# One new order of finer stages in the attention phase of a hybrid encoder block

## What is computed

```
h = rms_norm(x); q, k, v, p = h @ W_in              # 512, 128, 128, 512 columns
q, k = rms_norm(q), rms_norm(k)                     # per head of 64
a = attention(q, k, v, sinks)                       # window of 128, chunks of 64, a sink per head
m = (trailing means of p over 2, 4, 8, 16, minus p) @ pool_w, scaled
x = x + concat([a, m]) @ W_out
u = causal_conv3(rms_norm(x) @ W_up)                # 2 x 2816 columns
x = x + (silu(u_gate) * u_value) @ W_down
```

## Time and profile before

| | us |
|---|---|
| median of 3 executions | 1937.17 (1935.85 to 1940.52) |
| profiled execution | 1936.87 |
| its span, first to last instruction | 1935.0 |
| TensorE busy | 1788.9, 92% of the span |
| VectorE busy | 1350.6, 70% |
| ScalarE busy | 872.2, 45% |
| GpSimd busy | 244.5, 13% |
| mean granted TensorE clock | 0.966 |

### The profile page before, as it was taken

How to read it: one execution, slowest core, us unless ns; L and a number is a source line. 1 busy time by engine, 2 the same in 40 slices (tenths; PEclk the granted TensorE clock), 3 DMA queues, 4 the chain that set the end, 5 groups by cost and what they waited for, 6 DMA issues and landing times.

```text
span 1935.0 us, 23457 instructions
## 1 busy us (share of the span) xinstructions
PE 1788.9 (92%) x8490; PEld 1488.2 (77%) x8490; DVE 1350.6 (70%) x1786; ACT 872.2 (45%) x1499; POOL 244.5 (13%) x278
## 2 busy tenths in 40 slices
PE   5779979979976599999999999999999899999999
PEld 5668867768865488888888788888887688888887
DVE  4464454454532698989998889888897777775784
ACT  5454563663553444444445444444443433333331
POOL 1211211211111300000000000000001212220110
PEclk9989989989988699999999999999999899999999
DMA  5232244234443434243235622222223799885884
GB/s 182 66 124 72 66 163 142 66 121 141 142 154 139 151 132 142 68 140 120 88 122 192 227 91 77 88 77 87 85 79 112 261 377 318 288 296 174 295 298 148
DMA packets 218563, 295.51 MB, mean 153 GB/s; under 512 B 12937, under 2 KB 120145, under 8 KB 218449
## 3 DMA queue, kind: packets, MB, share of 16 engines
q1 hardware_dynamic: 199009, 239.49, 38.4%
q10 hardware_dynamic: 19440, 54.53, 7.2%
HBM read 234.20 MB, written 59.77 MB: 152 GB/s over the span
## 4 chain that ended last, share of the span: by engine, by line
PE 71%; DMA 9%; DVE 8%; ACT 7%; issue 3%; POOL 1%; SPq 1%; ACTq 0%; DVEq 0%; POOLq 0%
PE ps L625 23%; PE ps L627 23%; PE ps L626 23%; DMA dg<-gT_d 4%; ACT xs L972 2%; DMA h2T_d<-hs 1%; DMA dw<-in_w_down_dram 1%; ACT junk L884 1%; PE ps L663 1%; ACT n L896 1%; DVE ds_lo L1554 1%; DVE cb L1439 1%; DMA x_d<-r 1%; ACT r L1004 1%; ACT w_hi L866 1%
## 5 line engine op out<-in xcount | busy, mean ns | idle before, releaser
L625 PE MATMUL ps<-va_hi,wv 128*128 128x512 f32 x1232 | 483.5, 392 | 46.3 <-DVE va_lo L1387 30.8
L627 PE MATMUL ps<-va_hi,wv 128*128 128x512 f32 x1232 | 482.4, 392 | 0.0
L626 PE MATMUL ps<-va_lo,wv 128*128 128x512 f32 x1232 | 482.3, 391 | 0.0
L625 PEld LDWEIGHTS ps<-va_hi,wv 128*128 128x128 f32 x1232 | 233.4, 189 | 96.5 <-DVE va_lo L1387 31.7
L627 PEld LDWEIGHTS ps<-va_hi,wv 128*128 128x128 f32 x1232 | 233.1, 189 | 49.0
L626 PEld LDWEIGHTS ps<-va_lo,wv 128*128 128x128 f32 x1232 | 233.5, 190 | 48.4
L625 PE MATMUL ps<-dt_hi,ds_hi 128*128 128x512 f32 x616 | 239.7, 389 | 0.1
L627 PE MATMUL ps<-dt_hi,ds_lo 128*128 128x512 f32 x616 | 239.6, 389 | 0.0
L626 PE MATMUL ps<-dt_lo,ds_hi 128*128 128x512 f32 x616 | 239.6, 389 | 0.0
L1439 DVE SCALAR_TENSOR_TENSOR cb<-ub,cst,cb 128x1024 f32<-128x1024 f32 x176 | 218.8, 1286 | 7.5 <-ACT cb L1069 7.5
L1202 DVE TENSOR_TENSOR w_lo<-raw,w_hi 128x1024 fp32r<-128x1024 f32 x72 | 96.4, 1348 | 136.4 <-ACT w_hi L866 135.9
(11 more groups left out here) (158 smaller groups left out, 2923.1 us busy)
## 6 DMA issues: line engine op xcount, KB each, us to landing
dg<-gT_d SPq DMA_DIRECT2D x264, 256.0 KB, 5.0
rw<-in_w_up_dram SPq DMA_DIRECT2D x84, 512.0 KB, 5.1
dw<-in_w_down_dram SPq DMA_DIRECT2D x132, 256.0 KB, 5.4
gT_d<-cb ACTq DMA_DIRECT2D x44, 512.0 KB, 2.6
raw<-in_w_in_dram SPq DMA_DIRECT2D x40, 512.0 KB, 3.8
raw<-in_w_out_dram SPq DMA_DIRECT2D x32, 512.0 KB, 3.9
n<-in_x_dram SPq DMA_DIRECT2D x16, 512.0 KB, 5.8
x_d<-r ACTq DMA_DIRECT2D x16, 512.0 KB, 3.2
```

What stands on the lines that cost most here:

```text
L625: pe.matmul(out_ap, l_hi, r_hi, start=first, stop=False, skip_group_check=True)
L626: pe.matmul(out_ap, l_hi, r_lo, start=False, stop=False, skip_group_check=True)
L627: return pe.matmul(out_ap, l_lo, r_hi, start=False, stop=last, skip_group_check=True)
```

## The change

`ORDER` is written anew. n1 and n2 become two stages each: n1sq, n2sq (squares, stores, inverse roots) and n1sc, n2sc (the scaling, now `tensor_scalar` on VectorE). t1 is taken in halves and t2 in quarters j of two feature tiles. The inverse sums leave s for a stage inv; ScalarE's copy of sp is a stage pt; the key and value work of kv is a stage kve. join waits for o(1, 1) instead of o(1, 3). The first block is turned tile by tile into all eight banks as each tile is scaled, and its products start after one feature tile instead of five. o waits for the attention half only at k = 2. VectorE adds before it splits. The seven small vectors are loaded from ScalarE's queue instead of SP's.

```diff
     units("n1", 0, ())
-    units("t1", 0, ())
+    units("t1", 0, (0,))
     for g in range(4):
...
             units("win", 0, (g,))
+    units("kv", 0, (0,), (1,))
+    units("kve", 0, ())
     for a in range(NB):
         more, back = a + 1 < NB, a > 0
-        units("kv", a, (0,), (1,))
+        if a > 1:
+            units("kv", a, (0,))
+            units("t2", a - 2, (2,))
+            units("kv", a, (1,))
+            units("kve", a, ())
+            units("t2", a - 2, (3,))
+        units("q", a, (0,))
         units("pm", a, (0,), (1,))
         units("win", a, (2,))
-        units("q", a, (0,))
+        if more:
+            units("n1sq", a + 1, ())
+        units("q", a, (1,))
         units("pm", a, (2,))
         units("win", a, (3,))
-        units("q", a, (1,), (2,))
+        if more:
+            units("n1sc", a + 1, ())
+        units("q", a, (2,))
         units("pm", a, (3,))
...
             units("kt", a, ())
-            units("n1", a + 1, ())
-            units("t1", a + 1, ())
+            units("t1", a + 1, (0,), (1,))
             units("qt", a, ())
...
             units("win", a + 1, (0,))
+            units("inv", a, (0,))
             units("pin", a + 1, (1,))
+            units("s", a, (2,), (3,))
             units("win", a + 1, (1,))
-            units("s", a, (2,), (3,))
             units("pin", a + 1, (2,))
+            units("inv", a, (1,))
+            units("pin", a + 1, (3,))
             units("sp", a, (0,), (1,))
-            units("pin", a + 1, (3,))
+            units("pt", a, (0,), (1,))
+            units("kv", a + 1, (0,))
             units("av", a, (0,), (1,))
             units("sp", a, (2,), (3,))
+            units("pt", a, (2,), (3,))
+            units("kv", a + 1, (1,))
             units("av", a, (2,), (3,))
+            units("kve", a + 1, ())
             continue
...
         units("o", a - 1, (1, 0))
-        if more:
-            units("n1", a + 1, ())
+        units("inv", a, (0,))
         units("o", a - 1, (1, 1))
         units("s", a, (2,), (3,))
+        units("join", a, ())
         units("o", a - 1, (1, 2), (1, 3))
-        units("join", a, ())
+        units("inv", a, (1,))
         if more:
-            units("t1", a + 1, ())
-            units("n2", a - 1, ())
+            units("t1", a + 1, (0,))
+            units("sp", a, (0,))
+            units("t1", a + 1, (1,))
+            units("sp", a, (1,))
+            units("pt", a, (0,), (1,))
             units("pin", a + 1, (0,))
-            units("sp", a, (0,), (1,))
+            units("n2sq", a - 1, ())
             units("win", a + 1, (0,))
+            units("av", a, (0,), (1,))
             units("pin", a + 1, (1,))
-            units("av", a, (0,), (1,))
+            units("n2sc", a - 1, ())
             units("win", a + 1, (1,))
+            units("sp", a, (2,), (3,))
+            units("pt", a, (2,), (3,))
             units("pin", a + 1, (2,))
-            units("sp", a, (2,), (3,))
+            units("av", a, (2,), (3,))
+            units("t2", a - 1, (0,))
             units("pin", a + 1, (3,))
-            units("t2", a - 1, ())
-            units("av", a, (2,), (3,))
-        else:
-            units("sp", a, (0,), (1,))
-            units("av", a, (0,), (1,))
-            units("sp", a, (2,), (3,))
-            units("n2", a - 1, ())
-            units("av", a, (2,), (3,))
+            units("t2", a - 1, (1,))
     last = NB - 1
-    units("o", last, (0, 0), (0, 1))
-    units("t2", last - 1, ())
+    units("sp", last, (0,), (1,))
+    units("pt", last, (0,), (1,))
+    units("n2sq", last - 1, ())
+    units("o", last, (0, 0))
+    units("n2sc", last - 1, ())
+    units("av", last, (0,), (1,))
+    units("sp", last, (2,), (3,))
+    units("pt", last, (2,), (3,))
+    units("o", last, (0, 1))
+    units("av", last, (2,), (3,))
+    units("t2", last - 1, (0,), (1,))
+    units("o", last, (0, 2))
+    units("t2", last - 1, (2,), (3,))
     units("first_weights", 0, ())
-    units("o", last, (0, 2), (0, 3))
+    units("o", last, (0, 3))
     units("first_variant", 0, ())
     units("o", last, (1, 0), (1, 1), (1, 2), (1, 3))
-    units("n2", last, ())
-    units("t2", last, ())
+    units("n2sq", last, ())
+    units("n2sc", last, ())
+    units("t2", last, (0,), (1,), (2,), (3,))
     return o
...
+def t1_bank(a, dt):
+    return (4 + dt) % 8 if a == 0 else 4 + dt % 4
+def t2_bank(a, dt):
+    return {NB - 2: dt % 4, NB - 1: 4 + dt % 4}[a] if a >= NB - 2 else 4 + dt % 2
+def t2_lag(a):
+    return 4 if a >= NB - 2 else 2
...
-            for row, a, src in [(0, 0, conv_w[0, 0:2].rearrange("c (f p) -> (c f) p", p=P)),
...
-                sp.dma_start(vec_rows[row:row + src.shape[0], a, :], src).then_inc(vectors_in, 16)
...
-            def t1(a):
+            def t1(a, h):
                 if a == 0:
...
-                for dt in range(KT):
-                    bank = T1_BANK + dt % 4
+                    for t in range(NT):
+                        pe.wait_ge(S["xs1"], t + 1)
+                        for dt in range(KT):
+                            tr = pe.transpose(ps[:, t1_bank(0, dt), tokens(t)], n1[:, t, dt * P:(dt + 1) * P], ident[:])
+                            if t == NT - 1:
+                                tr.then_inc(S["turned1"], 1)
+                    return
+                for dt in range(4 * h, 4 * h + 4):
+                    bank = t1_bank(a, dt)
                     if dt < 4 and a == 1:
...
                         pe.wait_ge(S["m_copied"], 4)
-                    elif dt < 4 and a > 1:
+                        pe.wait_ge(S["k_scaled"], 2)
+                    elif dt < 4:
                         pe.wait_ge(S["out_added"], 8 * (a - 2) + 4 + dt + 1)
-                    elif dt >= 4:
+                    else:
                         pe.wait_ge(S["hT_lo"], KT * a + dt - 3)
...
                 pe.wait_ge(S["split_lo"], n + 1)
-                pe.wait_ge(S["hT_lo"], KT * a + 4 + g + 1)
+                pe.wait_ge(S["hT_lo"], KT * a + g + (1 if a == 0 else 5))
...
-                    if g == 0 and k > 4:
+                    if g == 0 and k > (0 if a == 0 else 4):
                         pe.wait_ge(S["hT_lo"], KT * a + k + 1)
...
                         pe.wait_ge(S["p_copied"], 4 * a + 4)
-                        wait(pe, "h2_copied", KT * (a - 1))
...
                         pe.wait_ge(S["mT_ready"], 4 * a + 4)
-                        pe.wait_ge(S["aT_lo"], NT * a + NT)
                         if a + 1 < NB:
...
                         pe.wait_ge(S["k_scaled"], 2 * (a + 1) + t - 1)
+                if h == 0 and k == 2:
+                    pe.wait_ge(S["aT_lo"], NT * a + NT)
...
-            def t2(a):
-                for dt in range(KT):
-                    bank = T2_BANK(a) + dt % 4
-                    if dt >= 4:
-                        pe.wait_ge(S["h2_copied"], KT * a + dt - 3)
+            def t2(a, j):
+                for dt in (2 * j, 2 * j + 1):
+                    if dt >= t2_lag(a):
+                        pe.wait_ge(S["h2_copied"], KT * a + dt - t2_lag(a) + 1)
                     elif a + 2 < NB:
                         pe.wait_ge(S["p_copied"], 4 * (a + 2) + dt + 1)
-                    elif a + 2 == NB:
-                        wait(pe, "aT_lo", NT * NB)
+                    elif a + 1 < NB:
+                        pe.wait_ge(S["aT_lo"], NT * NB)
                     else:
...
-                        mm = pe.transpose(ps[:, bank, tokens(t)], r[:, t, dt * P:(dt + 1) * P], ident[:])
+                        mm = pe.transpose(ps[:, t2_bank(a, dt), tokens(t)], r[:, t, dt * P:(dt + 1) * P], ident[:])
                     mm.then_inc(S["turned2"], 1)
...
+            for row, a, src in [(0, 0, conv_w[0, 0:2].rearrange("c (f p) -> (c f) p", p=P)),
...
+                act.dma_start(vec_rows[row:row + src.shape[0], a, :], src).then_inc(vectors_in, 16)
...
-            def n1_(a):
+            def n1sq(a):
                 for t in range(NT):
...
                     square(0, a, t, n1)
-                if a == 0:
-                    for n in range(LEAD):
-                        split(n)
-                for t in range(NT):
-                    act.wait_ge(S["rstd1"], NT * a + t + 1)
-                    a_.activation(n1[:, t, :], n1[:, t, :], ACT.Copy, scale=rstd[0][:, t:t + 1]).then_inc(S["xs1"], 1)
-            def t1(a):
+            def n1_(a):
+                n1sq(a)
+                for n in range(LEAD):
+                    split(n)
+            def t1(a, h):
                 if a == 0:
                     act.wait_ge(vectors_read, 1)
-                else:
+                elif h == 0:
                     act.wait_ge(S["unit_used"], used("q", a - 1, 3))
-                for dt in range(KT):
+                for dt in range(KT) if a == 0 else range(4 * h, 4 * h + 4):
                     act.wait_ge(S["turned1"], KT * a + dt + 1)
...
```

(75 more changed lines are left out.)

30 lines of the change are left out of this document (14 added, 16 removed).

## The result

The changed kernel takes 1880.49 us (median of 4 runs, 1876.05 to 1884.66), the kernel before 1938.85 in the same comparison (4 runs, 1935.85 to 1940.83): a ratio of 0.970, 95% interval 0.967 to 0.973. The forecast was 1867, its range 1850 to 1888. So the direction and most of the size were right, and the result lies inside the stated range; the point was 13 us too low, and the forecast's narrower range of 1857 to 1877 missed by 3.5.

The account below looks back on a forecast made before the run. The first phase was taken as bound by TensorE with holes from queue order, which also lower the clock. Seven terms, 7.0 + 8.0 + 10.8 + 33.4 + 3.2 + 6.4 + 1.1 = 69.9, took 1936.9 to 1867 us; range 1850 to 1888.

Parts of the forecast that it names:

- 1, the start: Up to and just behind the first product: VectorE scaling, tile-by-tile turning and starting after one feature tile save 7.0 us.
- the rival on turning: Runs of turning in the first phase: the clock falls to 1.2 GHz there, giving 1880 us; chance 12%.
- 7, the crossing: Crossing to the second phase: only the scaling changes, from ScalarE to VectorE, saving 1.1 us.
- 2, block 0's middle: Middle of block 0: the 11.0 us wait for block 1's norm moves under q, saving 8.0 us.
- 3 and 4, block 0's attention and the middle blocks: Block 0's attention and two middle blocks: most idle time and missing clock go, saving 10.8 and 33.4 us.
- step 5: Three waits on mix_lo of 1.1 us each, covered by the q unit put in between, saving 3.2 us.
- 6, the last block: Last block, to 605.23 us: idle and missing clock shrink despite new holes, the largest for r's load, saving 6.4 us.
- Splits didn't fall behind: Rival for all 72 weight units: splits come late and stop TensorE, 2 us a unit, giving 2011 us; chance 3%.
- Late neighbours: Rival for ScalarE's and VectorE's queues: new neighbours some 3 us late at ten first-phase places, giving 1897 us; chance 8%.

Follow-up runs that it names:

- the run with three edits: Changed kernel with first values ahead of the scaling of r, block 2's turning all before the third output unit, next block's squares one unit later: 1863.0 us.
- the runs with three and four edits: Changed kernel with first values before r's scaling, r turned earlier, squares one unit later: 1863.0 us; the fourth edit adds SyncE's later loads: 1859.16 us.

## Why the prediction came out as it did

**1, the start: the number right, 7.1 for 7.0 us, and in part by luck.** The terms up to the first product make 4.6 + 3.0 + 1.8 - 0.2 = 9.2, and the trace gives 7.1. The 32 turnings ran from 11.11 to 16.98 us, 0.18 each, where the step took 0.11 for them. On the other side stand two losses behind the first product, 0.5 for the pace of the low parts and 1.7 for a lower clock. Neither is there: the products follow each other every 0.23 us from the first one on, as they do in the kernel before and later in the block, so at the full clock. No run shows the 1.7, here or in the price of the rival on turning.

**7, the crossing: right** as far as it can be told, 0.9 for 1.1. TensorE's wait for the scaled `r` fell from 7.8 to 6.3 us, but the crossing as a whole differs by over 1 us between runs that don't touch it.

**2, block 0's middle: 1.6 too much.** The 11.0 us wait for the norm went, and the hole of 4.2 us for the low parts of the turned block stands in the trace at 4.2. TensorE's busy time is the same (66.4 and 66.1 us), as forecast, where slow turning and a slower clock cancelled. What is missing is idle time: the wait on `mix_lo` stays at 1.3 us, where 1.1 was to go, and the turning of the keys waits 1.9 us for a query norm instead of 1.1. In the run with three edits, with the squares one unit later, the first is gone and the second back at 1.1.

**3 and 4, block 0's attention and the middle blocks: right** in mechanism and size, 47.1 us for 47.4 (with 3.2 of step 5). In the two middle blocks idle fell by 26.2 us, where 25.5 follow from the forecast, and TensorE's busy time by 9.8, where the clock was to give 10.0. The blocks are 125.0 and 127.1 us where 125 to 128 was said. The first low part stands TensorE 0.8 us, for which 0.85 was worked out. That a large part comes from the norm's place is shown by the run with the norm alone (21.4 us over the whole kernel). Join early and the inverses together add some 12, with and without it; the inverses alone lose.

**5, the waits on `mix_lo`: not as said.** They fell only from 4.5 to 3.7 us. The cover that the extra query unit gives is taken by the squares now standing in front of ScalarE's split, with VectorE's split in front of the window sums. With the squares one unit later, in the runs with three and four edits, no such wait is left.

**6, the last block: the step that failed,** -2.6 us instead of 6.4, 9.0 of the 13 us. The prediction put "2.8 (av's low parts stand behind n2sc on VectorE, which waits for the store of `r`)". The place is right, and it is 9.9 us. Two things were missing. The step counted what waits for the stores but not what runs beside them: by the new order they come 9 us earlier against the end of block 2 and SyncE's loads for the dense phase 12 us later, so the two share the DMA engines (8.6 us a store for 3.2). The run with the loads later gives 4.3 us of the hole back. And in that run the hole is still 5.6 us, twice the 2.8, and faster stores would not shrink it: GpSimd's inverse roots, which stand behind its work on the probabilities, come no earlier than the last store; the step doesn't name GpSimd. With the values ahead of the scaling 8.6 us of the hole go, whatever holds the scaling. The other large term, 6.1 us for the load of `r`, was 7.1. Together idle is 18.4 us, where the terms of this step make 11.6: 6.8 of the 9.0. The other 2.2 are the lower clock that comes with the holes (TensorE busy 59.75 us, where 57.5 were left).

**The range** held the result with luck. Its upper end was set for a lower clock in the turnings, a slow scaling and a poor start; none of them came, and the excess that did come was the last block's.

**The scaling on VectorE:** 0.748 us each, and 0.68 from one start to the next:

```profile
L1260 DVE TENSOR_SCALAR n<-n,rstd x16: 739/748/781, 10.2 to 289.2; 128x1024 f32<-128x1024 f32 x16
L1260 DVE TENSOR_SCALAR r<-r,rstd x16: 745/748/755, 243.7 to 552.7; 128x1024 f32<-128x1024 f32 x16
```

0.83 was taken, and 0.42 to 1.22 held it. The estimate from the Trainium skill, VectorE: DVE Perf Modes, section "Mode 2×_2P — use both read ports for one tensor", was 0.53 us plus a fixed part. The trace leaves 0.2 for that part, so it agrees. ScalarE's busy time fell by 35.2 us (34 said), VectorE's rose by 17.6 and not by 27: the 32 scalings add 22.0 by the line groups, and one group of the dense phase is 4.4 us shorter in this execution (ds_lo, 79.4 for 83.8).

**The rivals.** The clock didn't fall in the runs of turning: the 48 transposes between the output stage and the next products took 7.4 us in each middle block, with one wait of 0.8, and the granted clock is 1.00 over them. That the result lies at the 1880 us of this rival is chance. The Trainium skill, TensorE: Matmul & The Clock Gate, section "Part 4: PE-mode transpose", says that the full clock doesn't engage for transposes; these blocks disagree, as the earlier trace rows did. Splits didn't fall behind: TensorE's waits up to 640 us name no w_lo. Late neighbours did appear, but in one block and at two places rather than ten, and with the squares at `mix_lo`.

## What to carry to other kernels

When a step is moved, write down for every queue, SyncE's too, when its transfers are issued in the new order: two that lay 16 us apart can fall together, and a store at three times its time holds whatever waits for its buffer. Put an instruction that waits for a DMA behind the last one in its queue that something else needs; then it matters little what else the instruction waits for. Swapping two steps that TensorE needs one right after the other only passed the wait on (13.9 to 11.7 us at one place, 5.5 to 7.3 at the next); work taken out of the queue ahead of the last release (a whole norm under another stage) shortened it. Don't judge one part of a new order by itself: the inverses alone lost 9.6 us, and with join moved too the pair won 12.8.

## What the runs showed of the hardware

A 512 KB store took 3.2 us alone and 8.6 beside six loads of 512 KB, while the DMA engines moved 377 GB/s. A cast of 512 columns on VectorE takes 0.36 us in a row of four, and 1.2 us while GpSimd multiplies a tile of 1024 columns (1.42 and 4.78 us for four). Five operations with PSUM operands ran beside the same work of GpSimd in the run with join early (`hT_lo`, 3.41 us for five) and were no slower: 0.68 each, where eight of them took 5.59 us, 0.70 each, with GpSimd idle in the kernel before. GpSimd there:

```profile
248.76 3.75 POOL L1636 TENSOR_TENSOR xs<-xs,row_sum 128x1024 f32<-128x1024 f32 x2 [17.36 <-DVE row_sum L1334]
```
